# A streaming encoder layer on one core: value split moved behind the LayerNorm squares, row scaling and two divisions given to ScalarE, the last out-projection steps taken tile by tile, one more buffer place for the weights

## The reference

```python
def rmsnorm(x, g):
    y = x * lax.rsqrt(jnp.mean(x * x, axis=-1, keepdims=True) + EPS)
    return y * g

h = rmsnorm(x, g_pre_mix)
q, k, v, u, g = split_projection(h, w_in)          # u = u_a * sigmoid(u_b), g = sigmoid(...)
attn = sliding-window attention of q, k, v (window 128 + own chunk of 64, sinks, relative bias)
y = causal depthwise conv of u (width 31); y = silu(layernorm(y, ln_g, ln_b)); conv = y @ w_pw
m = g[..., 0] * attn + g[..., 1] * conv
x = x + rmsnorm(m @ w_out, g_post_mix)
h = rmsnorm(x, g_pre_ffn)
f = (silu(h @ w_ffn_gate) * (h @ w_ffn_up)) @ w_ffn_down
y = x + rmsnorm(f, g_post_ffn)
```

## Time and profile before

| | |
|---|---|
| median of 3 runs | 3098.47 us (3096.92 to 3100.09) |
| the profiled execution | 3105.38 us, of which the span of its instructions is 3103.6 us |
| TensorE busy | 3021.6 us (97%) |
| VectorE, ScalarE, GpSimd busy | 1550.6, 1056.2 and 608.4 us |
| mean granted TensorE clock | 0.991 of full speed |

### The profile page before, as it was taken

The page is one execution under the profiler, slowest core; times in us unless marked ns, Lnnn a source line. Parts: engine busy times, 40 slices in busy tenths (PEclk is TensorE's granted clock), DMA queues, the critical chain, the costliest instruction groups (busy, mean ns, idle before and its releaser), DMA issues.

```text
span 3103.6 us, 42640 instructions
## 1 busy us (share of the span) xinstructions
PE 3021.6 (97%) x16775; PEld 2589.2 (83%) x16775; DVE 1550.6 (50%) x2785; ACT 1056.2 (34%) x1953; POOL 608.4 (20%) x597
## 2 busy tenths in 40 slices
PE   8989989999999999999999999999999999999998
PEld 7767778888887878888887888888899999899976
DVE  8987755555797730003497652002379665300023
ACT  5766432234355520003155532002235443200012
POOL 4962110000481000000085000000048200100001
PEclk9999999999999999999999999999999999999999
DMA  7865667787654355556655454556555434455543
GB/s 284 277 226 199 232 242 291 292 299 288 228 193 150 137 204 190 190 193 214 217 191 176 137 203 163 193 197 215 187 202 177 144 132 171 144 170 175 173 166 131
DMA packets 173160, 620.10 MB, mean 200 GB/s; under 512 B 20528, under 2 KB 23344, under 8 KB 172448
## 3 DMA queue, kind: packets, MB, share of 16 engines
q1 hardware_dynamic: 172000, 616.96, 57.0%
q10 hardware_dynamic: 960, 0.40, 0.0%
HBM read 478.05 MB, written 139.33 MB: 199 GB/s over the span
## 4 chain that ended last, share of the span: by engine, by line
PE 80%; DVE 3%; DMA 2%; ACT 1%; POOL 1%; issue 1%; SPq 0%; ACTq 0%; POOLq 0%; DVEq 0%
PE PS L891 54%; PE PS L951 6%; PE PS L952 6%; PE PS L953 6%; PE PS L925 2%; PE PS L1082 1%; PE PS L1053 1%; DVE PS L1659 1%; PE PS L1041 1%; PE PS L870 1%; DMA out_y_prompt<-x 1%; PE PS L949 0%; POOL sq_sum L812 0%; DMA u<-in_state 0%; PE PS L950 0%
## 5 line engine op out<-in xcount | busy, mean ns | idle before, releaser
L891 PE MATMUL PS<-h_hi,w_hi 128*128 128x512 f32 (+2 forms) x3328 | 1062.2, 352 | 14.1 <-DVE u L1945 8.4
L891 PE MATMUL PS<-h_lo,w_hi 128*128 128x512 f32 (+2 forms) x3328 | 1053.7, 350 | 0.0
L891 PE MATMUL PS<-h_hi,w_lo 128*128 128x512 f32 (+2 forms) x3328 | 1053.2, 349 | 0.0
L891 PEld LDWEIGHTS PS<-h_hi,w_hi 128*128 128x128 f32 x3328 | 590.6, 189 | 98.4 <-issue 21.6
L891 PEld LDWEIGHTS PS<-h_hi,w_lo 128*128 128x128 f32 x3328 | 590.5, 189 | 78.6
L891 PEld LDWEIGHTS PS<-h_lo,w_hi 128*128 128x128 f32 x3328 | 590.8, 189 | 76.9 <-issue 1.7
L797 POOL TENSOR_TENSOR y<-y,prod 128x512 f32<-128x512 f32 (+1 forms) x333 | 430.5, 1320 | 161.2 <-ACT prod L1359 147.9
L1659 DVE SCALAR_TENSOR_TENSOR PS<-u,dw,PS 128x512 f32<-128x512 f32 (+1 forms) x604 | 434.6, 774 | 7.1
L2106 DVE TENSOR_TENSOR f<-PS,tmp 128x512 f32<-128x512 f32 (+1 forms) x88 | 61.6, 700 | 676.8 <-PE PS L891 657.4
L1496 ACT ACTIVATE tmp<-PS 128x512 f32<-128x512 f32 (+1 forms) x88 | 52.9, 601 | 670.5 <-PE PS L891 650.6
L951 PE MATMUL PS<-w_hi,f_hi 128*128 128x512 f32 x704 | 275.4, 391 | 1.4 <-ACT ostash_d L1316 1.1
(11 more groups left out here) (245 smaller groups left out, 3618.9 us busy)
## 6 DMA issues: line engine op xcount, KB each, us to landing
w_lo<-lo_dram SPq DMA_DIRECT2D x372, 512.0 KB, 4.5
w_hi<-hi_dram SPq DMA_DIRECT2D x372, 512.0 KB, 3.6
w_raw<-in_w_stream SPq DMA_DIRECT2D x124, 512.0 KB, 3.8
hi_dram<-w_hi SPq DMA_DIRECT2D x124, 512.0 KB, 3.7
lo_dram<-w_lo SPq DMA_DIRECT2D x124, 512.0 KB, 3.6
x<-in_x_prompt SPq DMA_DIRECT2D x4, 2048.0 KB, 12.2
xs<-in_x_prompt SPq DMA_DIRECT2D x12, 512.0 KB, 5.6
out_y_prompt<-x SPq DMA_DIRECT2D x3, 2048.0 KB, 10.6
```

The costliest lines, as they stand in the source:

```text
L891: last = nc.tensor.matmul(PS[:, k0 + off, col:col + n], w, x[:, k, c0:c0 + n], start=first and k == 0, stop=stop and k == KT - 1)
```

## The change

- `HI` goes from 3 to 4 and `LO` from 4 to 5: one more place for high parts and one more for low and raw parts. Every load, split and release counts with them.
- The copies and splits of the values on ScalarE and VectorE move from step `S_A`+1 to `value_step(b)`, which is `S_A`+4 in block 0 and `S_A`+2 in the others, behind the squares. TensorE's turning stays. The variance in block 3 uses PSUM banks 4 and 5.
- In block 0 the divisions of attention units 0 and 1 are done by ScalarE (four instructions, Copy with a scale) instead of VectorE.
- The 17 row scalings of the norm between the halves go from VectorE to ScalarE (`scale_by_act`), with another order of the norm's work on all engines.
- `tail(b)` is 3 in block 0 and 4 in the others. TensorE turns tile 0 after tile 2 of the tail and tile 1 within or after tile 3; tiles 2 and 3 are turned among the first FFN half-steps.

```diff
-HI = 3
-LO = 4
+HI = 4
+LO = 5
...
+        def scaled(eng, n):
+            b = min(n // 8, NB - 1)
+            if n - 8 * b < tiles(b):
+                eng.wait_ge(hs_ok, first_norm(b, n - 8 * b) + 1)
+            else:
+                eng.wait_ge(hs_act_ok, first_norm(b, n - 8 * b - tiles(b)) + 1)
...
+        def value_step(b):
+            return S_A + ln_shift(b) + 5
+        def probs_by_act(b, n):
+            return b == 0 and n < 2
...
         def tail(b):
-            return 3 if b else 2
+            return 4 if b else 3
...
                     if s == S_F - 1:
                         post_inv_rms(b, 0, 0)
-                        for tt in range(1, tiles(b)):
-                            post_inv_rms(b, tt, 0)
-                            inv_rms(b, tt - 1, 1)
-                        inv_rms(b, tiles(b) - 1, 1)
+                        post_inv_rms(b, 1, 0)
+                        inv_rms(b, 0, 1)
+                        post_inv_rms(b, 2, 0)
+                        inv_rms(b, 1, 1)
+                        inv_rms(b, 2, 1)
+                        post_inv_rms(b, 3, 0)
...
+                        if tt == 3 and not ext(b) and s == steps[1]:
+                            transpose_tile(b, 1, 1)
                     if tt < tiles(b) - 1:
                         last.then_inc(o_done, 1)
+                    if tt == 2:
+                        transpose_tile(b, 0, 1)
+                    if tt == 3 and ext(b):
+                        transpose_tile(b, 1, 1)
...
             def var_bank(b):
-                return 6 if ext(b) else 3
+                return 4 if ext(b) else 3
...
                         if ln == 5:
-                            result_out(pe, b, S_A - 1)
                             channel_squares(b, ypieces)
...
                             out_tail(b)
-                            for tt in range(3):
-                                transpose_tile(b, tt, 1)
                             if ext(b):
-                                first_ffn_steps(b, (((0, YH, 0, T - YH), 1, {0: (3,), 1: (4,)}),
+                                first_ffn_steps(b, (((0, YH, 0, T - YH), 1, {0: (2,), 1: (3, 4)}),
                                                     ((YH, TX - YH, 1, 0), 4, {})))
                             else:
-                                first_ffn_steps(b, (((0, T // 2, 0, 0), 1, {1: (3,)}),
+                                first_ffn_steps(b, (((0, T // 2, 0, 0), 1, {0: (2,), 1: (3,)}),
                                                     ((T // 2, T // 2, 0, T // 2), 3, {})))
...
+            def scale_by_act(b, tt):
+                n, r = norm_tile(b, tt, 1), rows(tt)
+                act.wait_ge(rs_ok, n + 1)
+                if tt < 2:
+                    act.wait_ge(hlo_ok, n - 1)
+                else:
+                    act.wait_ge(tr_done, n - 1)
+                A(x_tile(b, tt, 1)[r, :], x1[r, tt, :], ACT.Copy, scale=rstd[r, n % 4:n % 4 + 1]).then_inc(hs_act_ok, 1)
...
+                if probs_by_act(b, n):
+                    act.wait_ge(rl_ok, gu + 1)
+                    for h in range(4):
+                        ph = probs_of(h, scores_from(b, n))
+                        ins = A(ph, ph, ACT.Copy, scale=rl[:, h:h + 1])
+                    ins.then_inc(p_act_ok, 1)
...
-                    if r == turn_step(b):
+                    if s == value_step(b):
                         act.wait_ge(vt_done, b + 1)
```

More of the change, by code:

```diff
@@ L644, in weights_at @@
             def weights_at(g):
[L646 removed]
+                if g + LO - 1 < NS:
                     load_raw(g + LO - 1)
@@ L709, in _ @@
                         sp.dma_start(u[:, :, HIST + T:UW - S], state).then_inc(state_in, 16)
-                    if ext(b) and s == turn_step(b) + 2:
+                    if ext(b) and s == value_step(b) + 1:
                         sp.wait_ge(win_ok, 4)
@@ L755, in inv_rms @@
                 if n >= 4:
-                    pool.wait_ge(hs_ok, n - 3)
+                    scaled(pool, n - 4)
                 link(nc.gpsimd.tensor_scalar(rstd[:, c:c + 1], ssq[:, c:c + 1], 1.0 / D, EPS,
@@ L858, in transpose_tile @@
                 n = norm_tile(b, tt, second)
-                pe.wait_ge(hs_ok, n + 1)
+                scaled(pe, n)
                 if not second and b and tt >= 2:
@@ L1564, in _ @@
                         sum_squares(b, 0, 1, 2)
+                        scale_by_act(b, 0)
                         post_squares(b, 2, 0, 1)
                         sum_squares(b, 1, 1, 3)
-                        post_squares(b, 3, 0, 2)
+                        normed_hi(b, 0, 1)
+                        scale_by_act(b, 1)
+                        sum_squares(b, 2, 1, 3)
                         if ext(b):
-                            sum_squares(b, 2, 1, 4)
+                            scale_by_act(b, 2)
+                            post_squares(b, 3, 0, 3)
+                            normed_hi(b, 1, 1)
                             post_squares(b, 4, 0, 3)
-                            for tt in range(3):
-                                normed_hi(b, tt, 1)
                             sum_squares(b, 3, 1, 5)
+                            scale_by_act(b, 3)
+                            normed_hi(b, 2, 1)
                             sum_squares(b, 4, 1, 5)
+                            scale_by_act(b, 4)
                             normed_hi(b, 3, 1)
@@ L1684, in sum_squares_of_tiles, with scale_rows @@
                 TT(sq_sum[:, 0:yw], sq_sum[:, 0:yw], first, ALU.add).then_inc(sq_summed, 1)
-            def scale_rows(b, tt, second):
-                n, r = norm_tile(b, tt, second), rows(tt)
+            def scale_rows(b, tt):
+                n, r = norm_tile(b, tt, 0), rows(tt)
                 dve.wait_ge(rs_ok, n + 1)
[L1690 to L1696, removed]
+                x = x_tile(b, tt, 0)[r, :]
+                nc.vector.tensor_scalar(x, x, rstd[r, n % 4:n % 4 + 1], None, ALU.mult).then_inc(hs_ok, 1)
             def gains_in(b, tt):
@@ L2001, in _ @@
                             n = piece.stop - piece.start
-                            ins = nc.vector.tensor_scalar(rs_bc[:, piece], PS[:, (6 if ext(b) else 3) + off, 0:n],
+                            ins = nc.vector.tensor_scalar(rs_bc[:, piece], PS[:, (4 if ext(b) else 3) + off, 0:n],
                                                           EPS, None, ALU.add)
@@ L2078, in _ @@
                     if s == S_F - 1:
[L2079 to L2083, removed]
+                        for tt in range(3):
+                            residual(b, tt, 0)
+                        normed_lo(b, 0, 1)
+                        normed_lo(b, 1, 1)
+                        residual(b, 3, 0)
                         if ext(b):
-                            residual(b, 3, 0)
-                            scale_rows(b, 2, 1)
-                            for tt in range(3):
-                                normed_lo(b, tt, 1)
                             residual(b, 4, 0)
-                            scale_rows(b, 3, 1)
-                            scale_rows(b, 4, 1)
-                            normed_lo(b, 3, 1)
-                            normed_lo(b, 4, 1)
-                        else:
-                            normed_lo(b, 0, 1)
-                            scale_rows(b, 2, 1)
-                            normed_lo(b, 1, 1)
+                        else:
                             split_lo(G(b, S_F + 1))
-                            residual(b, 3, 0)
-                            normed_lo(b, 2, 1)
-                            scale_rows(b, 3, 1)
-                            normed_lo(b, 3, 1)
+                        for tt in range(2, tiles(b)):
+                            normed_lo(b, tt, 1)
                     if kind == "ffn_up":
@@ L2123, in _ @@
                         if start is not None:
-                            scale_rows(b + 1, start, 0)
+                            scale_rows(b + 1, start)
                         if out is not None:
```

33 lines of the change are left out of this document (23 added, 10 removed).

## The result

| | before | changed |
|---|---|---|
| median | 3099.28 us (4 runs) | 3076.81 us (3074.33 to 3078.84, 4 runs) |
| profiled execution | 3105.38 us | 3074.33 us |
| granted clock in it | 0.991 | 0.997 |

The ratio is 0.9928 with a 95% interval of 0.9916 to 0.9940: 22.5 us faster by the medians, where 28.5 were forecast. 3076.81 lies in the range given, 3060 to 3087. One of the four runs of before took 3342.0 us and is not in the ratio; without it the median of before is 3098.47 us and the gain 21.7. The profiled pair is 31.1 us apart, more than the medians: it sets a long execution of before (the others on record go from 3093 to 3107 us) against the shortest of the four after.

What follows compares the result with a forecast made beforehand. TensorE, busy 97%, was taken as the bound, so only its waits and slow clock could be won. Seven terms summed to 28.5 us (11.5 to 39.3), taking 3098.47 to 3070.0 us, range 3060 to 3087.

Steps and rivals of the forecast that it cites:

- (d): Block 0, clock behind the waits at the channel sum and units 0 and 1: half the slow-clock cost goes, 3.0 us.
- (b): Block 0, values moved behind the squares: GpSimd's wait for ScalarE's last conv product leaves the channel sum's chain, 1.5 us.
- (c): Block 0 attention, divisions of units 0 and 1 by ScalarE: probabilities come sooner and VectorE is freed, 5.0 us.
- (g): Norm in blocks 1 to 3: most waits for scaled rows, low parts and weights from DRAM go, 6.8 us.
- (a): Start of block 0, one more place for weights: VectorE's wait for a high part goes, 1.5 us.
- (e): Variance in blocks 1 to 3: with values behind the squares, all of TensorE's variance waits go, 6.7 us.
- (f): Norm in block 0: longer tail covers it and VectorE loses four scalings; first full FFN step begins 4.0 us sooner.
- B: Rival: half the first part doesn't come, at block 0's channel sum, divisions and the variance; 3080 us, chance 0.21.
- B's sign at the gates: Sign of that rival: ScalarE shows in TensorE's list as the one waited for at the gates; no size given.
- C: Rival: ScalarE is the wrong engine for the norm's 17 scalings, 0.31 us dearer each; 3075 to 3083 us, chance 0.09.
- D: Rival: nothing measurable changes; only the ring's 1.5 and the loads' 2.9 us come, 3094 us, chance 0.05.
- E: Rival: slower, scalings of tiles 2 and 3 stand late on ScalarE after the tail, 9.0 us a block; 3106, chance 0.03.

Runs made afterwards that it cites:

- ScalarE's wait: Changed kernel, but in block 0's attention ScalarE's split of a high part waits one step longer for TensorE, as with three places; 3068.52 us, ratio 0.9902.
- GpSimd's wait: Changed kernel, but in block 0's attention GpSimd begins the low part only after VectorE has divided the probabilities of the unit (2 to 9); 3067.51 us, ratio 0.9892.
- values early: Changed kernel with the copies and splits of the values back at step S_A+1; 3083.33 us, ratio 0.9953.
- short tail: Changed kernel with tails of 2 steps in block 0 and 3 in the others, as before; 3084.01 us, ratio 0.9950.
- scalings on VectorE: Changed kernel with the 17 row scalings of the norm on VectorE between its residuals, all else as changed; 3078.75 us, ratio 0.9934.

## Why the prediction was right, and where it was not

The direction and the range were right. The sum of 28.5 us left out a loss and had one term much too small. As measured below, the terms make 2.7 + 0.3 + 3.4 + 2.3 + 6.5 + 3.4 + 11.8 = 30.4 us, and the loss that the forecast put at nothing takes 8.0: 22.4, where some 22 were measured. So near a match is partly luck, for one term comes from medians and the others from single traces, and (d) lies partly within (b) and (c). That the 28.5 came within some 6 us is luck too: 5.0 us missing in (g) stood against the 8.0.

**What failed: the sentence in (c) that the same four instructions in unit 2 take only 1.11 us.** It was true of the kernel before, and I carried it over to the changed one; a longer division was in no term. I read the 3.28 against 1.11 as a property of units 0 and 1. It was one of the phase between GpSimd and VectorE, and term (a) moved that phase. The working of (a) counted the split's wait for a place as pure loss; in attention this same wait of 1.56 us held GpSimd's low part off the division. The change lost 8.0 us there between matmuls 1000 and 1600, and the run in which only this wait is back is 8.3 us faster. Without the collision the change brings 30 us (ScalarE's wait) to 33 (GpSimd's wait) against the forecast's 28.5. The Trainium skill (SBUF — State Buffer, the section on its two sides) has VectorE and GpSimd lock a common port for a whole instruction, and I cited it for two units only; the same rule spoke of every unit that would come to lie beside a low part. The traces agree with it: 3.1 us beside GpSimd, 1.11 apart from it, in the same order of instructions, and all of the difference in the one division of four that ends just behind the low part.

**(a) a place more at the start**, 1.5 forecast: the kernel before with that edit alone is 2.7 us ahead at matmul 600. (The changed kernel's 3.7 hold luck: matmul 200 starts between 43.5 and 46.3 us in executions whose kernels are alike up to there. Behind it the traces are steadier: from matmul 200 to 600 they take 98.4 and 99.0 us with three places and 96.2 to 96.6 with four.) Undersized, since ScalarE's earlier splits help at more than the one row I read.

**(b) values in block 0**, 1.5 forecast: undone, matmuls 700 to 800 take 32.0 us against 31.3 to 31.7 in six traces with the values late (30.2 in the changed kernel's own), so it loses 0.3 us or little more, and the channel sum's wait fell from 5.0 to 4.5. The 1.50 us of GpSimd's wait was not what bound the sum; which of its additions did was not tried.

**(c) divisions of units 0 and 1**, 5.0: 5.7 in the medians, 3.4 in the trace. Right in size. ScalarE takes 1.49 us for four:

```profile
224.03 1.49 ACT L1461 ACTIVATE pc<-pc,small 128x192 f32<-128x192 f32 x4 [0.44 <-DVE small L1856]
...
231.60 1.49 ACT L1461 ACTIVATE pc<-pc,small 128x192 f32<-128x192 f32 x4 [0.44 <-DVE small L1856]
```

But not beside GpSimd, as the forecast had it: ScalarE splits the next weight only behind its divisions, so that the low parts start at 226.55 and 234.11, when each group is done. It is the order on ScalarE that keeps them apart, and whether ScalarE would be slowed beside GpSimd no run here shows.

**(d) clock**, 3.0: by the windows, from 0.06 × 41 + 0.21 × 16 = 5.8 to 0.03 × 41 + 0.14 × 16 = 3.5 us, so 2.3. About right, though the windows no longer hold quite the same work. But it is luck in part, for the clock can go either way here: from 233 to 241 us it is 0.65 in the changed kernel's trace and 1.00 in three others (ScalarE's wait, values early, and both). From matmul 800 to 1000 those three take 40.5 us, the changed kernel 44.8, and three more with its order up to there, at 0.61 to 0.63, take 43.1.

**(e) variance**, 6.7: the waits are all gone, and undoing the move costs 6.5 us. Right, by its own mechanism.

**(f) norm of block 0**, 4.0: 3.4 (from 0.4 ahead to 3.8). Right in size, but not by the tail and the scalings alone: the kernel before with only the two places gains 2.2 here, and TensorE's 1.7 for ScalarE's `tmp` fall to 0.2 in it. The forecast had the places nowhere in this term. The short tail costs 2.7. TensorE's waits there are 3.6 for low parts, 0.9 for scaled rows, 0.6 and 0.2 for others, 5.3 instead of 7.9.

**(g) norms of blocks 1 to 3**, 6.8: 4.7 + 3.6 + 3.5 = 11.8 us in the profiled pair. The waits for scaled rows and low parts fell about as laid out by hand, to 6.0 us where 5.2 were to be left; what was left out is the clock behind them. In block 1, from 1130 to 1170 us, it was 0.91 before:

```profile
1130.00:1170.00 40.00, 36.23 (x205) 32.08 (x204) 17.52 (x16) 12.55 (x22) 7.01 (x20) 0.91 0.33 120
```

And it is 1.00, the full 2.4 GHz, after:

```profile
1130.00:1170.00 40.00, 38.13 (x252) 34.40 (x251) 14.19 (x12) 17.40 (x25) 5.78 (x17) 1.00 0.50 180
```

On 36.23 us of work that is up to 3.3 us of the 4.7. A pause of TensorE in these stages cost more than its length, and I had counted this in block 0 only. 4.8 of the 11.8 us come with the two places alone, where 2.9 were forecast for the loads. In blocks 1 and 2 the longer tail adds nothing, and scaling on VectorE costs 0.6 each; what is left there, some 1.8 us a block, goes by exclusion to the new order of the norm's work, which no run tried by itself.

**Rivals.** B's time was near (3080), and it named the right victim, block 0's part of the gain, but not the mechanism. TensorE waits for the divisions on ScalarE 2.3 us in two, but with those of units 0 and 1 on VectorE its waits for probabilities are 13.3 us instead of 8.9 and 2.3. Of B's sign at the gates there is a little: one wait for ScalarE's gate result in block 3 is 2.7 us after the change and was 2.1 before. C fell: the scaling is dearer on ScalarE, 1.15 us:

```profile
L1311 ACT ACTIVATE xs<-x,rstd 128x1024 f32<-128x1024 f32 x16 | 18.4, 1149 | 6.3 <-POOL rstd L776 6.1
```

That is the Trainium skill's estimate (ScalarE: Activation LUTs, rules for kernel authors) rather than the 1.06 of my nearest row; but on VectorE the kernel is no faster. (At this estimate C's mild end is 17 × 0.40 = 6.8 us, 3076.8 and not the 3076.5 of the forecast.) The Trainium skill's advice to multiply on VectorE would have won nothing here (1.9 us slower, within the intervals). D fell with the result, and E did not occur: the longest wait for scaled rows is 1.2 us.

## What to carry to other kernels

A wait that a change removes may have kept two engines apart. When an instruction shows two durations in one profile, ask what ran beside it in each case, and ask this of every edit that shifts the start of either, also of one that only adds a buffer, namely whether the slow case becomes the steady one. And compare traces at the same instruction, not by totals: the edit that measured as nothing held a loss of 8 us and a gain that paid for it.

## What the runs showed of the hardware that was not expected

The collision locks itself in. In the changed kernel VectorE's division and GpSimd's low part are both released by ScalarE's exp, the delay shifts the next unit as much as the next low part, and eight units in a row stay in it; a wait of 1.56 us in the right place keeps all of them out.

The clock behind the same pause is not always the same. From 233 to 241 us it is 1.00 in three traces in which TensorE waits 2.9 us from 193 to 241, and 0.62 and 0.63 in two in which it waits 3.0 and 2.8 (GpSimd's wait, scalings on VectorE). In block 3 one wait of 2.7 us for a gate result, at 2432 us in the changed kernel, has a clock of 1.00 behind it in the changed kernel and in the run with short tails, and of 0.79 and 0.83 in the runs with ScalarE's and GpSimd's wait; matmuls 11500 to 12400 take 115.9 us in the first two and 118.5 and 117.4 in the others. No run tells what decides it.

In block 3's FFN 1200 matmuls (14400 to 15600 in the trace's order) took 152.0 us in the profiled executions of before and of the run without divisions on ScalarE, and 150.0 in all ten others, at a granted clock of 1.00 in the window from 2700 to 2950 us of before and after alike. No run here tells why; it makes 3.3 of the 31.1 us between the two profiled executions.
